# Fourier mixing from sums and differences of the sequence's halves: even and odd frequencies apart, each from half as many tokens

## The chip, the cores and the metric

The kernel runs on one core of a Trainium2 chip, all in f32. The metric is the device time of one execution in microseconds. The program computes several transformer blocks in a row on a sequence of 512 latent and 256 context tokens; the change concerns one short stage of the first block.

## The reference, cut to what matters

```python
FOURIER_WIDTH = 512; FOURIER_GROUPS = 4; FOURIER_GROUP_DIM = 128

def fourier_mix(u):                      # u: the first 512 columns of h @ w_in
    B_, L, _ = u.shape
    ug = u.reshape(B_, L, FOURIER_GROUPS, FOURIER_GROUP_DIM).astype(jnp.float32)
    f = jnp.fft.fft2(ug, axes=(1, 3), norm='ortho').real
    return f.reshape(B_, L, FOURIER_WIDTH).astype(u.dtype)
```

It is called once for the latent tokens (L = 512) and once for the context tokens (L = 256). The real part of the two-dimensional transform is cos(tokens) times cos(channels) minus sin(tokens) times sin(channels), which the kernel makes with matrix multiplications against tables.

## The kernel before

Activations lie transposed: channels on the 128 partitions, tokens along the free axis, 512 latent and behind them 256 context tokens, T = 768 together. The kernel is a row of stages. Each has one program for each engine and ends with a barrier of all engines.

`even_in` projects the normed input (25 jobs in `EV_JOBS`, in an order written out by hand). A job of the kinds z, q, k, v, u, r is one output tile of 128 channels: 8 matmuls of 512 and 8 of 256 columns (L1336, L1337) into one of three pairs of PSUM banks, and one ScalarE copy of 768 elements into SBUF (L1377). Jobs of the kind vt turn a value tile around (L1326), and VectorE copies them out (L1419); jobs g make the gates, on which VectorE has a chain of running sums behind the last one (L1394 to L1402, L1496). Job j waits only until the result of job j − 3 has been copied out. The four u tiles are the input of the Fourier mixing. The SP queue loads the projection's weights into three slots at the head of the region W, and behind the last of them the tables of the Fourier stage (L1302), over the same slots.

`fourier` works on four groups of 128 channels. `channels(g)` multiplies each of the 6 token tiles of a group with the 128-point table (L1450: 6 matmuls of 256 columns, cos and sin side by side). ScalarE copies the result into `G` (L1482), one of two buffers. `tokens(g)` sums over the token tiles with the tables of the sequence (L1460, L1461 for the latent, L1463, L1464 for the context tokens) into banks 6 and 7, and VectorE copies those into `A` (L1489). The order on TensorE is

```python
channels(0); channels(1)
for g in range(4):
    tokens(g)
    if g + 2 < 4:
        channels(g + 2)
```

`tokens(g)` waits for ScalarE's copy of its own group and for VectorE's copy of group g − 1, because there is one pair of result banks. `gla_scan` follows.

Of the kernel before, what the change touches and what calls it, by code (L numbers as in the profile page):

```python
# [19 lines left out]
MUL, ADD, SUB = ALU.mult, ALU.add, ALU.subtract  # L20

P = 128
D = 1024
KD = D // P
LAT, CTX = 512, 256
T = LAT + CTX
# [921 lines left out]
def pair_banks(ps, b, n):  # L948

    return ps[:, 2 * b:2 * b + 2, :].rearrange("p a c -> p (a c)")[:, 0:n]  # L950
# [281 lines left out]
EV_U = BIG  # L1232
# [21 lines left out]

def fourier_tables(m):
    at, W = m["at"], OFF["W"]
    return {"cos_lat": at(W, 4, LAT), "sin_lat": at(W + 4 * LAT, 4, LAT), "cos_ctx": at(W + 8 * LAT, 2, CTX),
            "sin_ctx": at(W + 8 * LAT + 2 * CTX, 2, CTX)}


def even_in(nc, m, io, feed, norm, early, mods):
# [4 lines left out]
    st, s = stage(nc, "evi", Norm.SEMS + "wg mm act ab gm ex ln ls cu mid ep en vt vtc own g gp" + mods.SEMS, {**feed.sems})  # L1266
    ps, at, cols = m["ps"], m["at"], m["cols"]
    wg = at(EV_WG, 2, 256)
    z, q, k, v = at(EV_Z, T), at(EV_Q, 2, T), at(EV_K, 2, T), at(EV_V, 4, T)
# [3 lines left out]
    released, tiles = {}, {}  # L1273
# [9 lines left out]
    def chunks(n):  # L1283
        return cum[:, n, :].rearrange("p (a c) -> p a c", c=RW_C)

    with st, nc.Block() as block:
        @block.sync
        def _(sp):
            sp.dma_start(wg[0:16, :, :], io["w_gla_gate"].rearrange("d r n -> r d n")).then_inc(s["wg"], 16)
            mods.begin(sp, s)  # L1290
            feed.rest(m, sp, s["mm"], lambda w: mods.between(sp, s, 0, w))
            sp.dma_start(at(GL_DFT, 2 * P), io["dft128"]).then_inc(early["dft"], 16)
            for name, dst in fourier_tables(m).items():
                n = dst.shape[1] * dst.shape[2]
                lo = {"cos_lat": 0, "sin_lat": 4 * LAT, "cos_ctx": 8 * LAT, "sin_ctx": 8 * LAT + 2 * CTX}[name]
                if lo < feed.slots * KD * P:
                    sp.wait_ge(s["mm"], feed.last_over(lo, lo + n))
                if lo + n > feed.slots * KD * P:
                    sp.wait_ge(s["mdm"], mods.N)
                if lo + n > EV_WG - OFF["W"]:  # L1300
                    sp.wait_ge(s["gp"], 4)
                sp.dma_start(dst, io[name].rearrange("(k p) n -> p k n", p=P)).then_inc(early["tab"], 16)  # L1302
# [82 lines left out]
        @block.vector  # L1385
        def _(dve):
            norm.dve(dve, s)
            own = Count(dve, s["own"])

            def centre(n):  # L1390
                last = RW_C - 1 if n < 2 else 0
                dve.wait_ge(s["cu"], n + 1)
                x = chunks(n)
                own.link(dve.tensor_scalar(ref[:, n, :], x[:, :, RW_C // 2], 1.0, None, MUL))  # L1394
                own.link(dve.tensor_tensor(fall[:, n, :], x[:, :, last], ref[:, n, :], SUB))
                dve.tensor_tensor(x, x, ref[:, n, :].rearrange("p (a c) -> p a c", c=1).to_broadcast([P, RW_NC, RW_C]), SUB
                                  ).then_inc(s["mid"], 1)

            def sums():
                for n in range(4):  # L1400
                    dve.wait_ge(s["ln"], n + 1)
                    dve.tensor_tensor(q_hat[:, n, :], q_hat[:, n, :], cum[:, n, :], SUB).then_inc(s["ls"], 1)  # L1402
                    dve.wait_ge(s["ls"], n + 1)
                    running_sum(dve, m["rst64"], q_hat[:, n, :], cum[:, n, :], n // 2).then_inc(s["cu"], 1)
                    if n:
                        centre(n - 1)
                centre(3)

            for j, (kind, i) in enumerate(EV_JOBS):
                x = pair_banks(ps, j % 3, T)  # L1410
                if kind == "g":
                    dve.wait_ge(s["ab"], i + 1)
                    dve.tensor_scalar(q_hat[:, i, :], x, bias(i), 0.0, ADD, ALU.min).then_inc(s["gm"], 1)
                    if i == 3:
                        dve.wait_ge(s["gm"], 4)
                        sums()
                if kind == "vt":
                    dve.wait_ge(s["vt"], i + 1)
                    dve.tensor_copy(vt[:, i, :, :].rearrange("p a c -> p (a c)"), x).then_inc(s["vtc"], 1)  # L1419
            mods.add(dve, s, 0)  # L1420
            e = RW_NC - 1
            own.done(dve.tensor_tensor(step[:, 0:2, 0:e], fall[:, 0:2, 0:e], ref[:, 0:2, 1:e + 1], ADD))
            own.done(dve.tensor_tensor(step[:, 0:2, e:e + 1], fall[:, 0:2, e:e + 1], ref[:, 0:2, 0:1], ADD))
            own.done(dve.tensor_tensor(step[:, 2:4, 1:e + 1], fall[:, 2:4, 1:e + 1], ref[:, 2:4, 0:e], ADD))
            own.link(dve.memset(step[:, 2:4, 0:1], 0.0))
            dve.memset(m["misc"][:, 31:32], 0.0).then_inc(s["g"], 1)
            for n in range(4):
                dve.wait_ge(s["ep"], n + 1)
                dve.scalar_tensor_tensor(q_hat[:, n, :], q[:, n % 2, :], 64.0 ** -0.5, q_hat[:, n, :], MUL, MUL)
                dve.wait_ge(s["en"], n + 1)  # L1430
                dve.tensor_tensor(cum[:, n, :], k[:, n % 2, :], cum[:, n, :], MUL)
            mods.add(dve, s, 1)


def fourier(nc, m, early):

    st, s = stage(nc, "fft", "g gc o oc", early)
    at, ps, A = m["at"], m["ps"], m["A"]
    ev = at(EV_U, 4, T)
    t = fourier_tables(m)  # L1440
    f = at(GL_DFT, 2 * P)
    G = at(EV_G, 2, TT, 2 * P)
    with st, nc.Block() as block:
        @block.tensor
        def _(pe):
            def channels(g):
                if g >= 2:
                    pe.wait_ge(s["gc"], g - 1)
                for t in range(TT):
                    mm = pe.matmul(ps[:, 3 * (g % 2) + t // 2, (t % 2) * 256:(t % 2) * 256 + 256], ev[:, g, t * P:(t + 1) * P], f,  # L1450
                                   start=True, stop=True)
                mm.then_inc(s["g"], 1)

            def tokens(g):
                x = G[:, g % 2, :, :]
                pe.wait_ge(s["gc"], g + 1)
                if g:
                    pe.wait_ge(s["oc"], g)
                for k in range(4):
                    pe.matmul(ps[:, 6, :], x[:, k, 0:P], t["cos_lat"][:, k, :], start=(k == 0), stop=False)  # L1460
                    pe.matmul(ps[:, 6, :], x[:, k, P:2 * P], t["sin_lat"][:, k, :], start=False, stop=(k == 3))  # L1461
                for k in range(2):
                    pe.matmul(ps[:, 7, 0:CTX], x[:, 4 + k, 0:P], t["cos_ctx"][:, k, :], start=(k == 0), stop=False)  # L1463
                    mm = pe.matmul(ps[:, 7, 0:CTX], x[:, 4 + k, P:2 * P], t["sin_ctx"][:, k, :], start=False, stop=(k == 1))  # L1464
                mm.then_inc(s["o"], 1)

            pe.wait_ge(s["dft"], 16)
            channels(0)
            channels(1)
            pe.wait_ge(s["tab"], 4 * 16)  # L1470
# [5 lines that stand above are left out]
        @block.scalar  # L1476
        def _(act):
            for g in range(4):
                act.wait_ge(s["g"], g + 1)
                if g >= 2:  # L1480
                    act.wait_ge(s["o"], g - 1)
                act.activation(G[:, g % 2, :, :].rearrange("p t c -> p (t c)"),  # L1482
                               ps[:, 3 * (g % 2):3 * (g % 2) + 3, :].rearrange("p a c -> p (a c)"), ACT.Copy).then_inc(s["gc"], 1)

        @block.vector
        def _(dve):
            for g in range(4):
                dve.wait_ge(s["o"], g + 1)
                dve.tensor_copy(A[:, g, :], pair_banks(ps, 3, T)).then_inc(s["oc"], 1)  # L1489


def running_sum(dve, reset, src, dst, backward):
# [2272 lines left out]
def shape_constants():  # L3765

    import numpy as np
    i = np.arange(P)
# [7 lines left out]
    g = np.arange(NE)  # L3776
# [7 lines left out]
    a = 2 * np.pi * np.outer(np.arange(P), np.arange(P)) / P  # L3784
    f["dft128"] = np.concatenate([np.cos(a), np.sin(a)], axis=1)
    for name, length in (("lat", LAT), ("ctx", CTX)):
        a = 2 * np.pi * (np.outer(np.arange(length), np.arange(length)) % length) / length
        f["cos_" + name] = np.cos(a) / np.sqrt(length * P)
        f["sin_" + name] = -np.sin(a) / np.sqrt(length * P)
    tok = np.arange(LAT)  # L3790
# [5 lines left out]
    i, j = i[:, None] % 64, np.arange(64)[None, :]  # L3796
# [82 lines left out]
```

## Time and profile before

| | |
|---|---|
| median of 3 runs | 3609.66 us (3606.34 to 3609.83) |
| span of the profiled execution | 3608.5 us |
| TensorE busy | 3331.8 us, 92% |
| VectorE busy | 1472.6 us, 41% |
| ScalarE busy | 920.5 us, 26% |
| GpSimd busy | 776.5 us, 22% |
| mean granted TensorE clock | 0.965 |
| projection and tables (`even_in`), about | until 261 us |
| Fourier stage | 262.1 to 311.2 us |

The profiled execution is given by its span, from its first to its last instruction; it has no other time of its own in the profile. In the profile PE is a TensorE matmul, PEld its weight load, DVE is VectorE, ACT ScalarE, SP the queue that issues loads. An f32 matmul of the code is two records, each with its own weight load. "PEclk" is the clock that TensorE was granted, as a part of full speed. Matmul records overlap by their drain: the pace is read from start to start.

### The profile page before, as it was taken

The page shows a single profiled execution, that of the slowest core. Times are in us where ns is not written, and L with a number is a line of the kernel's source. Part 1 is how long each engine was busy: PE and PEld are TensorE (multiplying, and loading weights), DVE is VectorE, ACT ScalarE, POOL GpSimd, SP SyncE. Part 2 cuts the span into 40 slices and gives each one's busy share as a digit, 9 for nine tenths or more (in the row PEclk, how much of TensorE's full clock was granted, in tenths as well). Part 3 has the DMA queues.
Part 4 walks back from the last instruction along what each step waited for, and adds up shares of the span by engine and source line. Part 5 has one row for each costly group of instructions (what it writes and reads, how often), then busy time and mean ns, then how long its engine had stood idle before and what let it go on. Part 6 is the DMA issues. An engine that isn't in the chain of part 4 may idle for free. (4 is left out here: it accounts for less than half of the span.)

```text
span 3608.5 us, 67939 instructions
## 1 busy us (share of the span) xinstructions
PE 3331.8 (92%) x27542; PEld 2255.2 (62%) x27542; DVE 1472.6 (41%) x3002; ACT 920.5 (26%) x1782; POOL 776.5 (22%) x727
## 2 busy tenths in 40 slices
PE   7999999999999999999999599989988899999984
PEld 3557555555555687787865289965775466655543
DVE  1213443345322454445266834434455233333324
ACT  2122232222002343222121433234322122222211
POOL 0000332223510024335410000003311233333320
PEclk9999999999999999999999599989999999999996
DMA  5330133312111003532211000001102799999996
GB/s 225 123 112 25 48 124 155 148 51 83 56 39 65 30 13 140 226 136 103 84 59 36 0 4 4 4 17 53 65 26 81 284 357 357 358 360 349 359 386 233
DMA packets 97639, 485.23 MB, mean 134 GB/s; under 512 B 16915, under 2 KB 21043, under 8 KB 53249
## 3 DMA queue, kind: packets, MB, share of 16 engines
q1 hardware_dynamic: 80880, 443.66, 33.4%
q0 software_dynamic: 16528, 38.25, 3.2%
q8 instruction: 176, 2.88, 0.3%
q14 instruction: 55, 0.44, 0.0%
HBM read 466.90 MB, written 31.46 MB: 138 GB/s over the span
## 5 line engine op out<-in xcount | busy, mean ns | idle before, releaser
L1011 PE MATMUL psum<-arena 128*128 128x384 f32 (+1 forms) x2464 | 674.4, 434 | 6.3 <-ACT arena L600 5.3
L1011 PEld LDWEIGHTS psum<-arena 128*128 128x128 f32 x2464 | 463.7, 189 | 221.3 <-issue 23.8
L842 PE MATMUL psum<-arena 128*128 128x256 f32 (+1 forms) x1904 | 511.6, 431 | 23.3 <-PEq L3092 10.0
L842 PEld LDWEIGHTS psum<-arena 128*128 128x128 f32 x1904 | 363.6, 191 | 171.8 <-issue 27.3
L3623 PE MATMUL psum<-arena 128*64 128x256 f32 x3072 | 352.6, 378 | 15.8 <-DMA arena<-exp_w_in 13.2
L3623 PEld LDWEIGHTS psum<-arena 128*64 128x64 f32 x3072 | 231.8, 134 | 161.4 <-issue 54.1
L453 POOL TENSOR_TENSOR arena<-arena 128x512 f32<-128x512 f32 x66 | 88.0, 1334 | 1054.9 <-POOLq L1671 365.7
L1139 DVE SCALAR_TENSOR_TENSOR arena<-arena 128x511 f32<-128x511 f32 (+1 forms) x264 | 177.0, 713 | 138.1 <-ACT arena L1117 135.0
L1089 ACT ACTIVATE arena<-psum 128x384 f32<-128x384 f32 (+1 forms) x176 | 76.3, 435 | 510.5 <-PE psum L1011 510.1
L462 POOL TENSOR_TENSOR arena<-arena 128x512 f32<-128x512 f32 (+1 forms) x74 | 114.6, 1549 | 395.6 <-PE psum L1011 245.6
L3637 PE MATMUL psum<-arena 128*64 128x512 f32 x768 | 185.3, 601 | 0.6 <-DMA arena<-exp_w_in 0.6
L1133 DVE TENSOR_TENSOR arena<-psum,arena 128x384 f32<-128x384 f32 (+1 forms) x132 | 64.6, 490 | 283.3 <-PE psum L1011 283.3
L2478 ACT ACTIVATE arena<-psum 128x256 f32<-128x256 f32 (+1 forms) x264 | 104.0, 422 | 240.2 <-PE psum L2327 62.1
L2796 PE MATMUL psum<-arena 128*128 128x384 f32 (+1 forms) x560 | 161.3, 449 | 4.1 <-ACT arena L600 4.0
L3717 DVE SCALAR_TENSOR_TENSOR arena<-arena,psum 128x128 f32<-128x128 f32 (+1 forms) x97 | 33.8, 349 | 281.0 <-ACT arena L3674 281.0
L563 POOL TENSOR_TENSOR arena<-arena 128x1536 f32<-128x1536 f32 (+1 forms) x3 | 11.3, 3766 | 636.3 <-ACT arena L600 636.3
L2796 PEld LDWEIGHTS psum<-arena 128*128 128x128 f32 x560 | 106.6, 191 | 59.5 <-ACT arena L600 7.9
L1336 PE MATMUL psum<-arena 128*128 128x512 f32 x272 | 140.7, 598 | 1.1 <-ACT arena L600 1.1
L3545 POOL TENSOR_TENSOR arena<-arena 128x1 f32<-128x1 f32 x195 | 39.8, 204 | 394.0 <-DVE arena L3712 379.4
L2039 PE MATMUL psum<-arena 128*128 128x512 f32 x240 | 116.6, 592 | 0.8 <-ACT arena L600 0.8
L2527 DVE TENSOR_TENSOR arena<-psum,arena 128x256 f32<-128x256 f32 x128 | 53.6, 424 | 130.7 <-PE psum L2459 39.5
L3562 POOL DMA_INDIRECT yrows<-arena x96 | 98.5, 1026 | 37.3 <-issue 37.3
(516 smaller groups left out, 5199.3 us busy)
## 6 DMA issues: line engine op xcount, KB each, us to landing
arena<-exp_w_in SPq DMA_DIRECT2D x207, 1024.0 KB
arena<-w_mod_r_in SPq DMA_DIRECT2D x72, 1024.0 KB, 7.0
arena<-w_ffn_up_in SPq DMA_DIRECT2D x44, 1024.0 KB, 4.8
arena<-w_ffn_down_in SPq DMA_DIRECT2D x32, 704.0 KB, 4.2
arena<-yrows SPq DMA_DIRECT2D x8, 2048.0 KB, 16.5
arena<-w_hgrn_in SPq DMA_DIRECT2D x10, 1024.0 KB
arena<-w_even_in_in SPq DMA_DIRECT2D x17, 512.0 KB, 3.6
arena<-w_in_in SPq DMA_DIRECT2D x15, 512.0 KB, 3.6
```

Source lines behind the costliest of these rows:

```text
L453: pool.tensor_tensor(s1, a21, a22, ADD).then_inc(s["ws"], 1)
L462: pool.tensor_tensor(a12, a12, self.piece(m, p, 5), SUB).then_inc(s["ws"], 1)
L842: mm = pe.matmul(pair_bank(ps, q, x, h), lhsT[:, k, :], rhs[:, k, :], start=(k == 0 and x in (1, 2, 7)), stop=(k == KH - 1), skip_group_ch ...
L1011: return pe.matmul(pair_bank(ps, q, x, h), feed.weights(m, q, x)[:, k, :], b.moving(x)[:, k, :], start=(k == 0 and x in (1, 2, 7)), stop=( ...
L1139: last = dve.scalar_tensor_tensor(y, x[:, lo + a:hi + e], column(q, v, tap), y, MUL, ADD)
L1336: pe.matmul(ps[:, 2 * b, :], lhsT, m["A"][:, x, 0:LAT], start=(x == 0), stop=(x == KD - 1))
L2039: mm = pe.matmul(ps[:, 2 * b, :], lhsT, m["A"][:, k, 0:LAT], start=(k == 0), stop=(k == KD - 1))
L2478: return act.activation(dst, src, ACT.Copy)
L2796: mm = pe.matmul(pair_bank(ps, i, x, h), lhsT[:, k, :], rhs[:, k, :], start=(k == 0 and x in (1, 2, 7)), stop=(k == 3), skip_group_check=x ...
L3562: pool.indirect_dma_start(io["yrows"], bass.IndirectOffsetOnAxis(ap=ids[:, u:u + 1].bitcast(U32), axis=0), y[u], None, bounds_check=LAT * ...
L3623: mm = pe.matmul(ps[64 * c:64 * c + 64, 0, 0:256], xt[u][:, k, :], wgu[w][:, k, :, c * P:(c + 1) * P], start=(k == 0), stop=(k == KD - 1))
L3637: mm = pe.matmul(ps[64 * c:64 * c + 64, 4, :], hT[:, j * 64:(j + 1) * 64], wdn[w][:, j, c * 512:(c + 1) * 512], start=(j == 0), stop=(j == 1))
```

## The change

The sequence's halves are combined before the transform. For even frequencies the kernel of the transform has the same value at tokens n and n + L/2, for odd ones the opposite value; so the even frequencies are a transform of the sum of the two halves, and the odd ones of their difference, each over L/2 tokens.

Behind the projection of each u tile VectorE writes the difference of the halves over the second half and then 2 x first half − difference, which is the sum, over the first half, for the latent and for the context tokens. The tables keep half of the rows, and their columns are sorted, the even frequencies first. `channels` is as it was: the transform over channels works on sums and differences alike. `tokens` makes the even frequencies from the tiles of sums and the odd ones from the tiles of differences. The copy out becomes two instructions, one for the latent and one for the context tokens, which write with a step of two elements and so put even and odd frequencies back in their order.

```diff
 def fourier_tables(m):
     at, W = m["at"], OFF["W"]
-    return {"cos_lat": at(W, 4, LAT), "sin_lat": at(W + 4 * LAT, 4, LAT), "cos_ctx": at(W + 8 * LAT, 2, CTX),
-            "sin_ctx": at(W + 8 * LAT + 2 * CTX, 2, CTX)}
+    return {"cos_lat": at(W, 2, LAT), "sin_lat": at(W + 2 * LAT, 2, LAT), "cos_ctx": at(W + 4 * LAT, 1, CTX),
+            "sin_ctx": at(W + 4 * LAT + CTX, 1, CTX)}
...
-                lo = {"cos_lat": 0, "sin_lat": 4 * LAT, "cos_ctx": 8 * LAT, "sin_ctx": 8 * LAT + 2 * CTX}[name]
+                lo = {"cos_lat": 0, "sin_lat": 2 * LAT, "cos_ctx": 4 * LAT, "sin_ctx": 4 * LAT + CTX}[name]
                 if lo < feed.slots * KD * P:
                     sp.wait_ge(s["mm"], feed.last_over(lo, lo + n))
                 if lo + n > feed.slots * KD * P:
...
                         sums()
+                if kind == "u":
+                    u = at(EV_U + i * T, T)
+                    dve.wait_ge(s["act"], tiles["u", i] + 1)
+                    for lo, mid, hi in ((0, LAT // 2, LAT), (LAT, LAT + CTX // 2, T)):
+                        own.link(dve.tensor_tensor(u[:, mid:hi], u[:, lo:mid], u[:, mid:hi], SUB))
+                        dve.scalar_tensor_tensor(u[:, lo:mid], u[:, lo:mid], 2.0, u[:, mid:hi], MUL, SUB)
                 if kind == "vt":
...
-                for k in range(4):
-                    pe.matmul(ps[:, 6, :], x[:, k, 0:P], t["cos_lat"][:, k, :], start=(k == 0), stop=False)
-                    pe.matmul(ps[:, 6, :], x[:, k, P:2 * P], t["sin_lat"][:, k, :], start=False, stop=(k == 3))
-                for k in range(2):
-                    pe.matmul(ps[:, 7, 0:CTX], x[:, 4 + k, 0:P], t["cos_ctx"][:, k, :], start=(k == 0), stop=False)
-                    mm = pe.matmul(ps[:, 7, 0:CTX], x[:, 4 + k, P:2 * P], t["sin_ctx"][:, k, :], start=False, stop=(k == 1))
+                for name, bank, first, tiles, half in (("lat", 6, 0, 2, LAT // 2), ("ctx", 7, 4, 1, CTX // 2)):
+                    for odd in range(2):
+                        part = slice(odd * half, (odd + 1) * half)
+                        for k in range(tiles):
+                            for j, table in enumerate(("cos_", "sin_")):
+                                mm = pe.matmul(ps[:, bank, part], x[:, first + odd * tiles + k, j * P:(j + 1) * P],
+                                               t[table + name][:, k, part], start=(k == 0 and j == 0),
+                                               stop=(k == tiles - 1 and j == 1))
                 mm.then_inc(s["o"], 1)
...
                 dve.wait_ge(s["o"], g + 1)
-                dve.tensor_copy(A[:, g, :], pair_banks(ps, 3, T)).then_inc(s["oc"], 1)
+                for bank, lo, hi in ((6, 0, LAT), (7, LAT, T)):
+                    o = dve.tensor_copy(A[:, g, lo:hi].rearrange("p (j a) -> p a j", a=2),
+                                        ps[:, bank, 0:hi - lo].rearrange("p (a j) -> p a j", a=2))
+                o.then_inc(s["oc"], 1)
...
     for name, length in (("lat", LAT), ("ctx", CTX)):
-        a = 2 * np.pi * (np.outer(np.arange(length), np.arange(length)) % length) / length
+        order = np.concatenate([np.arange(0, length, 2), np.arange(1, length, 2)])
+        a = 2 * np.pi * (np.outer(np.arange(length // 2), order) % length) / length
```

`own.link` sends an instruction and makes VectorE wait until it has finished.

## Rows read from the trace of the kernel before

**Rows 1.** The page, busy time and share of each engine:

```profile
PE 3331.8 (92%) x27542; PEld 2255.2 (62%) x27542; DVE 1472.6 (41%) x3002; ACT 920.5 (26%) x1782; POOL 776.5 (22%) x727
```

**Rows 2.** Timeline of TensorE in the Fourier stage: start, length, line, form, records:

```profile
262.15 7.00 PE L1450 MATMUL psum<-arena 128*128 128x256 f32 x24 [1.64 <-PEq L1286]
268.99 1.02 PE L1460 MATMUL psum<-arena 128*128 128x512 f32 x2
...
277.59 2.75 PE L1450 MATMUL psum<-arena 128*128 128x256 f32 x12
280.19 1.02 PE L1460 MATMUL psum<-arena 128*128 128x512 f32 x2
...
299.55 0.59 PE L1464 MATMUL psum<-arena 128*128 128x256 f32 x2
301.29 1.10 PE L1460 MATMUL psum<-arena 128*128 128x512 f32 x2 [1.14 <-DVE arena L1489]
...
312.55 0.45 PE L1571 MATMUL psum<-arena 64*64 64x64 f32 x8 [2.43 <-DVE arena L1649]
```

**Rows 3.** Timeline of ScalarE and VectorE in the Fourier stage:

```profile
269.19 1.45 ACT L1482 ACTIVATE arena<-psum 128x1536 f32<-128x1536 f32 x1 [1.14 <-PE psum L1450]
...
300.18 0.96 DVE L1489 COPY arena<-psum 128x768 f32<-128x768 f32 x1 [10.24 <-PE psum L1464]
```

**Rows 4.** Stretches of time: length, each engine's busy time, granted clock, DMA share, GB/s:

```profile
262.00:264.00 2.00, 1.85 (x5) 1.52 (x6) 0.00 (x0) 0.00 (x0) 0.00 (x0) 0.50 1.01 369
264.00:266.00 2.00, 2.00 (x8) 1.65 (x7) 0.00 (x0) 0.00 (x0) 0.00 (x0) 0.66 1.01 365
266.00:268.00 2.00, 2.00 (x11) 1.75 (x10) 0.00 (x0) 1.41 (x1) 0.00 (x0) 1.00 0.59 195
300.00:302.00 2.00, 0.86 (x3) 0.49 (x3) 0.96 (x1) 0.00 (x0) 0.00 (x0) 1.00 0.00 0
312.00:314.00 2.00, 1.45 (x34) 1.45 (x36) 0.79 (x3) 0.55 (x2) 0.00 (x0) 0.79 0.52 111
1225.00:1325.00 100.00, 99.98 (x678) 82.63 (x677) 55.05 (x122) 58.45 (x99) 0.00 (x0) 1.00 0.00 1
```

**Rows 5.** Timeline of TensorE in the attention stage:

```profile
1230.85 1.50 PE L1901 MATMUL psum<-arena 128*128 128x128 f32 x12
1232.19 1.02 PE L1892 MATMUL psum<-arena 128*128 128x512 f32 x2
```

**Rows 6.** Groups of VectorE instructions by line and form: busy us, mean ns:

```profile
L1646 DVE TENSOR_TENSOR arena<-arena 128x256 f32<-128x256 f32 x24 | 10.1, 421 | 6.2 <-PE psum L1593 6.2
L1633 DVE TENSOR_TENSOR arena<-psum,arena 128x128 f32<-128x128 f32 x24 | 6.9, 289 | 1.8 <-PE psum L1574 1.3
L3359 DVE TENSOR_TENSOR arena<-arena 128x256 f32<-128x256 f32 x1 | 0.5, 507 | 0.0
L3345 DVE TENSOR_TENSOR arena<-arena 128x256 f32<-128x256 f32 x1 | 0.4, 427 | 0.0
L3365 DVE COPY arena<-psum 128x64 f32<-128x64 f32 x1 | 0.2, 226 | 2.3 <-PE psum L3234 2.3
L1489 DVE COPY arena<-psum 128x768 f32<-128x768 f32 x4 | 3.8, 958 | 46.2 <-PE psum L1464 46.2
```

**Rows 7.** Timeline of VectorE and ScalarE in the projection:

```profile
179.76 0.96 DVE L1396 TENSOR_TENSOR arena<-arena 128x768 f32<-128x768 f32 x1
182.99 0.81 ACT L1377 ACTIVATE arena<-psum 128x768 f32<-128x768 f32 x1 [11.62 <-PE psum L1337]
185.46 0.96 DVE L1419 COPY arena<-psum 128x768 f32<-128x768 f32 x1 [4.74 <-PE psum L1326]
...
198.47 0.96 DVE L1419 COPY arena<-psum 128x768 f32<-128x768 f32 x1 [12.05 <-PE psum L1326]
```

**Rows 8.** Timeline of the SP queue at the projection's end:

```profile
258.09 0.39 SPq L1302 DMA_DIRECT2D arena<-cos_lat_in  x1
...
259.63 0.66 SPq L1302 DMA_DIRECT2D arena<-sin_ctx_in  x1
```

## The prediction

> **What bounds the kernel now.** I began with the page's busy shares: TensorE is busy for 92% of the span [rows 1], so work taken off its queue shows in the end unless something else ends last in its stage. The stage to look at is the Fourier mixing, 262 to 311 us. Its TensorE timeline [rows 2] is a straight line of instructions: 24 channel passes, then four times the token sums (one group of them 268.99 to 277.59), with the channel passes of groups 2 and 3 between. Every f32 multiplication stands there as two passes, so "x2" is one matmul of the code. The reader is to see that a line starts as the one before it runs out: TensorE waits for nobody, except ahead of the last group, where it stands from the end of group 2 to 301.29 for the VectorE copy that empties the two result banks. The other two engines are short next to it: the ScalarE copy of a group is 1.45 us, the VectorE copy 0.96 us [rows 3]. The granted clock is 0.50 when the stage begins, 1.00 from 266 us on, and stays 1.00 through the gap at 300 to 302 [rows 4]. So the stage is bound by the columns that TensorE streams. Its stages are closed by barriers: what it ends earlier, all later stages begin earlier.
>
> **Token sums: fewer columns.** One group now streams 8 matmuls of 512 columns and 4 of 256, that is 16 passes of 512 and 8 of 256, in 277.59 − 268.99 = 8.60 us [rows 2]. After the change the number of matmuls is the same, 12, and each has half the columns: 16 passes of 256 and 8 of 128. Their prices stand in the trace with the same 128x128 weights. The 12 channel passes of 256 columns run from 277.59 to 280.19, 0.217 us each [rows 2]; 12 passes of 128 columns in the attention stage run from 1230.85 to 1232.19, 0.112 us each [rows 5]. A group is then 16 x 0.217 + 8 x 0.112 = 3.47 + 0.89 = 4.36 us, 4.24 us less, and four groups give 16.96 us. The question is whether the weight load, which does not shrink (24 loads of 128x128 a group, before and after), sets a floor. A row says where it lies: 0.112 us at 128 columns is more than half of 0.217, but by little, so at 256 columns the load is covered, and at 128 just about. If on the contrary it took a 256-column time for each 128-column pass, the 32 such passes would cost 32 x (0.217 − 0.112) = 3.4 us more; that is the upper bound of this term.
>
> TensorE: Matmul & The Clock Gate, in the Trainium skill, section Back-to-back issue gap, speaks against the halving: it gives sustained pairs of load and matmul at about 81 ns for 128 columns where the bare matmul would be 56, because the load has to be paid as well. Taken as a factor of 1.45 on the bare half of my 256-column pass (an estimate), a 128-column pass would be 0.157 us and the change 32 x 0.045 = 1.4 us dearer; the row with 0.112 us is this kernel's own and is what the sum uses.
>
> **The order around them.** I followed the new schedule from the rows. Token sums 0 begin at 268.99 as now and end at 273.35. Channel passes 2 take 2.60 us, to 275.95; the ScalarE copy of group 1 is over at 270.64 [rows 3], so token sums 1 start at once. The copy of group 2 waits for its channel passes (275.95) and for token sums 0, and is over by 277.6, long before token sums 2 at 282.9; that of group 3 begins at about 282.9 and ends at 284.5, ahead of token sums 3 at 287.2 and later. So no ScalarE copy comes onto the path. Each copy has less room than before, but the least of it is over 2.5 us.
>
> **The copies out.** One VectorE copy of 768 elements (958 ns [rows 6]) becomes two, of 512 and 256, which write every second element so that even and odd frequencies interleave. From 958 ns at 768 and 226 ns at 64 elements [rows 6] an element is 1.04 ns and the fixed part 0.16 us: the pair costs 0.69 + 0.43 = 1.12 us, 0.16 more. Behind groups 0 and 1 it lies beside 2.60 us of channel passes, so nothing is seen; without that cover it would be twice 1.1 us. Behind groups 2 and 3 it is on the path: 2 x 0.16 = 0.32 us. The trace has no copy with a step of two elements. Nearest is L3359, which writes every third element: 507 ns for 256 where its neighbour with contiguous writes has 427 [rows 6], 0.31 ns an element. By that the pair is 0.24 us dearer, 0.48 for the two on the path. A gain is excluded, a step cannot be faster than none. I take 0.1 a copy, the lower side, since two elements' step is closer to the contiguous row, and keep 0 and 0.48 for the range.
>
> The Trainium skill, SBUF — State Buffer, section Door 1: The DMA port swizzle, says that lines are 16 bytes wide and that a stream runs at full rate while it hits a line at least twice. A step of two f32 hits twice, L3359's step of three does not always. By that the term is 0 here, against 0.48 by the row; the trace agrees as far as L3359 pays.
>
> **The new VectorE work in the projection.** For each of the four u tiles VectorE adds a difference and a sum over 256 elements, then the same over 128: 2 x 0.42 + 2 x 0.29 = 1.42 us [rows 6], with two short waits on itself about 1.5, so 6 us in all. I cost it at nothing. What hides it: VectorE's queue ends its running sums at about 180.7, u0 is long there, and the next thing behind it is the vt copy at 185.46, before which VectorE stands idle for 4.74 us. For u1 the ScalarE copy ends at 183.8, so VectorE is free again at about 185.3, just before that vt copy [rows 7]. The later u tiles repeat this every 13.0 us (185.46 to 198.47 [rows 7]). If it ran late by a few tenths, the vt copy would free a bank that TensorE wants only three projection tiles on, over 10 us later. And the stage's end is set by the last projection tile, done by 258.09 [rows 8]. Without that cover the cost would be those 6 us.
>
> **The tables.** The four loads were 2.5 MB, issued from 258.09 when the last projection tile is done [rows 8], and were still moving after 266 (DMA share 0.59 in 266 to 268 [rows 4]); the token sums want them at 268.99. They become 1.25 MB. The first now overwrites only the first weight slot and may go one tile earlier; the other three wait as before. All land sooner. Nothing was waiting for them, so the gain is 0; no queue has anything moved in front of it. Two of the waits that SP had there fall away, and SP has ended before the barrier either way.
>
> **The sum.** 16.96 − 0.32 − 0.2 = 16.4 us. The profiled span of 3608.5 becomes 3592.1. The median of the runs, 3609.66, stands 1.2 above that span; the same difference on it gives 3593.2 us.
>
> **Rivals.** First, the narrow passes do not run at 0.112 us between weight loads of alternating tables: for it speaks that nothing in this stage streams 128 columns yet and that each pass meets a load as long as itself; against it, that the 12 of [rows 5] load new weights each pass too. Up to 3.4 us back: 3596.6. The rule of the Trainium skill quoted above, the same page and section, is a milder case of this rival.
>
> Second, the clock drops in the gap ahead of the last group. That gap is 1.3 us now and would be about 1.6; the clock held at 1.00 through it [rows 4], but after the gap of 2.43 us at the stage's end [rows 2] it is 0.79 in 312 to 314. Token sums 3 at half clock cost 4.36 us more: 3597.6. Against it stands also the attention stage, which with its 128-column passes has 1.00 for 100 us [rows 4].
>
> Third, on the other side: the clock does not rise at all in this stage and stays at its 1.2 GHz level, after shorter stretches of streaming than now. Then the token sums are 4 x 8.72 = 34.9 us against 34.4 now, channel passes 2 and 3 are 2.6 us dearer each, and the first 24 go from 6.84 to 24 x 0.433 = 10.4: 0.5 + 5.2 + 3.6 + 0.5 for the copies = 9.8 us slower, 3619.5. It decides from the point at which some 16.4 us of full-speed work runs at half. Against it stands that the clock rises at 264 to 266 during the channel passes, which the change does not touch [rows 4].
>
> **How the numbers follow.** The forecast has 0.80, the first rival 0.06, the second 0.09, the third 0.02, and 0.03 lies with what I do not see. The predicted time is the forecast's. Its own range: the three runs spread over 3606.3 to 3609.8, so 3606.3 less 17 gives 3589.3, and 3609.8 less 15.9 (stepped writes at the full 0.48, no other loss) 3593.9. For such differences between runs I allow a little more: 3588 below. Above it reaches over both smaller rivals, 3596.6 and 3597.6, to 3599. A measurement of this kernel tells about 0.2%, 7.2 us, from no change; the forecast and the first two rivals are beyond that (3602.4), the third rival is slower.
>
> **What would show it.** The token lines should show 16 passes at 0.21 to 0.22 and 8 near 0.11 a group, some 4.4 us from the first to the next channel line; the two copies about 1.1 to 1.3 us together; the scan's first matmul near 296 instead of 312.55; the projection's TensorE line unchanged until 258; and the DMA quiet by 262 or so. The prediction is wrong if TensorE shows waits for VectorE inside the projection, if the granted clock after 270 is under 1.00, or if the copies run beyond 2 us.

## The result, and the profile after

| | before | after |
|---|---|---|
| median | 3608.0 us (3604.58 to 3609.83, 4 runs) | 3587.97 us (3585.96 to 3589.61, 4 runs) |
| ratio | | 0.9946, 95% interval 0.9934 to 0.9958 |
| span of the profiled execution | 3608.5 us | 3587.7 us |
| first channel pass to first matmul of the scan | 312.55 − 262.15 = 50.40 us | 295.75 − 262.11 = 33.64 us |

The four runs of the kernel before are the three that the forecast started from and one more. The change makes the kernel faster by about 0.5%. The forecast was 3593.2 us, a gain of 16.4 us. The Fourier stage itself gave 16.76 us; the spans of the two profiles differ by 20.8. So there are two questions: whether the stage went as forecast step by step, and where the other 4 us are from.

TensorE's timeline in the changed kernel, to be read beside [rows 2] (L1456 is the channel transform, L1470 the token sums, L1582 the scan's first line):

```profile
262.11 7.11 PE L1456 MATMUL psum<-arena 128*128 128x256 f32 x24 [1.64 <-PEq L1286]
269.06 4.51 PE L1470 MATMUL psum<-arena 128*128 128x256 f32 x24
273.41 2.76 PE L1456 MATMUL psum<-arena 128*128 128x256 f32 x12
276.00 4.51 PE L1470 MATMUL psum<-arena 128*128 128x256 f32 x24
280.35 2.76 PE L1456 MATMUL psum<-arena 128*128 128x256 f32 x12
282.95 4.51 PE L1470 MATMUL psum<-arena 128*128 128x256 f32 x24
288.67 4.59 PE L1470 MATMUL psum<-arena 128*128 128x256 f32 x24 [1.21 <-DVE arena L1498]
295.75 0.45 PE L1582 MATMUL psum<-arena 64*64 64x64 f32 x8 [2.49 <-DVE arena L1660]
```

The order is the same and no new wait has come. A group of token sums takes 273.41 − 269.06 = 4.35 us where it took 8.60. The only wait for VectorE is still that ahead of the last group.

A line names only one form of its group: 16 of the 24 passes have 256 columns, 8 have 128. The timeline cut late in group 0 shows the last seven of the 128-column passes by themselves:

```profile
272.63 0.94 PE L1470 MATMUL psum<-arena 128*128 128x128 f32 x7
273.41 0.38 PE L1456 MATMUL psum<-arena 128*128 128x256 f32 x1
```

That is 273.41 − 272.63 = 0.78 us for seven, 0.111 each.

VectorE's groups in the stage, by line and form (busy us, mean ns), and its timeline at one u tile of the projection, to be read beside [rows 6] and [rows 7]:

```profile
L1498 DVE COPY arena<-psum 128x512 f32<-128x512 f32 x4 | 2.8, 692 | 29.2 <-PE psum L1470 29.2
L1498 DVE COPY arena<-psum 128x256 f32<-128x256 f32 x4 | 1.7, 415 | 0.0
```

```profile
183.79 0.43 DVE L1421 TENSOR_TENSOR arena<-arena 128x256 f32<-128x256 f32 x1 [1.79 <-ACT arena L1377]
184.25 0.43 DVE L1422 SCALAR_TENSOR_TENSOR arena<-arena 128x256 f32<-128x256 f32 x1
184.60 0.28 DVE L1421 TENSOR_TENSOR arena<-arena 128x128 f32<-128x128 f32 x1
184.91 0.29 DVE L1422 SCALAR_TENSOR_TENSOR arena<-arena 128x128 f32<-128x128 f32 x1
185.42 0.96 DVE L1425 COPY arena<-psum 128x768 f32<-128x768 f32 x1 [0.21 <-PE psum L1326]
```

The four new instructions fill the 1.4 us between the end of ScalarE's copy and the vt copy, with 0.21 us of idle time left: the vt copy starts at 185.42 where it started at 185.46.

The SP queue (beside [rows 8]) and stretches of time (beside [rows 4]: length, busy time of PE, PEld, DVE, ACT, POOL, then the granted clock, DMA share, GB/s):

```profile
246.89 0.43 SPq L1302 DMA_DIRECT2D arena<-cos_lat_in  x1
258.06 0.37 SPq L1302 DMA_DIRECT2D arena<-sin_lat_in  x1
```

```profile
262.00:264.00 2.00, 1.89 (x7) 1.64 (x8) 0.00 (x0) 0.00 (x0) 0.00 (x0) 0.79 0.01 3
264.00:266.00 2.00, 2.00 (x7) 1.55 (x6) 0.00 (x0) 0.00 (x0) 0.00 (x0) 0.50 0.00 0
...
288.00:290.00 2.00, 1.33 (x6) 1.22 (x7) 0.53 (x2) 0.00 (x0) 0.00 (x0) 1.00 0.00 0
...
296.00:298.00 2.00, 2.00 (x56) 2.00 (x53) 1.01 (x3) 0.56 (x2) 0.00 (x0) 1.00 0.96 283
```

The DMA is quiet from 262 us on; in [rows 4] it was still at work after 266. The clock holds through the gap at 288 as it did before. The scan runs at full clock from its start, which it did not before: behind the row of 312 to 314 in [rows 4], the profile of the kernel before has

```profile
314.00:316.00 2.00, 2.00 (x23) 2.00 (x21) 0.72 (x2) 0.00 (x0) 0.00 (x0) 0.50 0.98 401
```

From the scan's first matmul to the first one of the stage behind it (L1677 before, L1688 after) it is 361.64 − 312.55 = 49.08 us before and 343.20 − 295.75 = 47.45 after, with the same instructions: 1.63 us. The remaining 2.3 us lie in the rest of the kernel, 3246.8 us before and 3244.5 after, which the change does not touch.

### The profile page after: what moved, and what is told of

Its sections match the earlier page's. It is cut to its first block and busy times, and to the rows that moved or that the text cites. A ratio compares the mean times of both kernels' runs of the same rounds, so it can differ in the third digit from the quotient of the medians.

```text
span 3587.7 us, 67958 instructions
## 1 busy us (share of the span) xinstructions
PE 3314.3 (92%) x27542; PEld 2250.5 (63%) x27542; DVE 1477.9 (41%) x3022; ACT 921.7 (26%) x1782; POOL 778.1 (22%) x727
```

## The experiments

Two theories on the part beyond 16.8 us, by the TensorE clock that was granted; a low stretch is one in which it was 0.50. **Theory A:** TensorE's low-clock stretches fall elsewhere in each execution, and the two profiles happened to differ. **Theory B:** the low stretch behind the Fourier stage belongs to the long stage, and the short one is rid of it for good. Beside them: is VectorE's new work really free, does the stepped write cost anything, and what is left in the stage.

**e1: the kernel before, profiled again.** No edit.

> The kernel before, unchanged, profiled a second time. Theory A (the part of the gain beyond the Fourier stage is the position of the granted clock's low stretches, different in each execution): the stages up to the Fourier stage's end agree with the first profile within 0.3 us except where a low stretch lies elsewhere, the low stretch at the start of the scan (313.1 to 316.6 in the first profile) may be there or not, and the span lies anywhere in 3604 to 3611. Theory B (the low stretch behind the Fourier stage belongs to the long stage of before): it is there again, at the same place within 1 us, and the scan stage is again about 44.4 us.

Measured: 3606.4 us over 10 runs beside 3606.23 over 21 (ratio 1.0, 0.9991 to 1.0009). Stage (first channel pass to the scan) 50.39, scan 49.08, as in the first profile, rest 3244.7. Theory B forecast this, and theory A allowed it. It also shows that the median of the kernel before over 21 runs is 3606.23: the median of the three runs that the forecast started from lay 3.4 us above that. (The expectations count the stages between other bounds: the 47.2 and 45.6 us of the scan there stand beside 49.08 and 47.45 here, and 50.0 and 33.3 us of the Fourier stage beside 50.40 and 33.64. The 44.4 us in the expectation of e1 fits neither count.)

**e2: the changed kernel, profiled again and timed five times.** No edit.

> The changed kernel, unchanged, profiled a second time and timed in five rounds. Both theories: the Fourier stage ends 16.8 us earlier than before (first matmul of the scan at 295.8 within 0.3 us, apart from clock). Theory A: the low stretches lie elsewhere than in the first profile of it, one may fall on the scan's start (then 297 to 301 runs at half clock and the scan stage is 1.6 us longer); the ratio over five rounds is about 1 - 16.8/3608 = 0.9953, a gain of 15 to 20 us. Theory B: the scan starts at full clock again and the ratio is about 0.9948 (18.5 us or more).

Measured: 3588.78 us (3587.78 to 3590.74) beside 3606.23, ratio 0.9953 (0.9939 to 0.9966), a gain of 17.4 us. The first 24 channel passes took longer here, at half clock until 268 us, so that the stage took 297.20 − 262.30 = 34.90 us; the scan 47.45. The ratio is the one that theory A gave, but its interval holds the 0.9948 of theory B too, so it decides nothing.

**e3: VectorE's new work alone**, in the kernel before:

```diff
+                if kind == "u":
+                    u, w = at(EV_U + i * T, T), at(EV_G, T)
+                    dve.wait_ge(s["act"], tiles["u", i] + 1)
+                    for lo, mid, hi in ((0, LAT // 2, LAT), (LAT, LAT + CTX // 2, T)):
+                        own.link(dve.tensor_tensor(w[:, mid:hi], u[:, lo:mid], u[:, mid:hi], SUB))
+                        own.link(dve.scalar_tensor_tensor(w[:, lo:mid], u[:, lo:mid], 2.0, w[:, mid:hi], MUL, SUB))
```

> The kernel before with nothing of the change but VectorE's sums and differences behind each u tile, written to a place that no one reads. Theory (hidden work): 0 us, the projection's TensorE timeline ends at 258.0 as before, ratio 0.9995 to 1.0005. Rival (it delays the copies of the turned value tiles and TensorE with them): up to 6 us later, ratio 1.0015.

Measured: 3606.49 us over 10 runs, ratio 1.0002 (0.9993 to 1.0011). The first channel pass stands at 262.11 (262.15 before), and TensorE has no wait from 170 to 258 us, as before. The work is hidden. And a surprise: this kernel has the long Fourier stage (51.69 us, a longer low stretch at its start), but its scan started at full clock and took 47.45 us:

```profile
313.80 0.45 PE L1577 MATMUL psum<-arena 64*64 64x64 f32 x8 [2.43 <-DVE arena L1655]
...
314.79 0.61 PE L1588 MATMUL psum<-arena 64*64 64x128 f32 x8
```

The same form took 1.07 us at half clock in e1:

```profile
312.38 0.45 PE L1571 MATMUL psum<-arena 64*64 64x64 f32 x8 [2.42 <-DVE arena L1649]
...
313.68 1.07 PE L1582 MATMUL psum<-arena 64*64 64x128 f32 x8
```

That is against theory B.

**e4: copies out without the step**, in the changed kernel; the frequencies are left unsorted.

```diff
-                    o = dve.tensor_copy(A[:, g, lo:hi].rearrange("p (j a) -> p a j", a=2),
-                                        ps[:, bank, 0:hi - lo].rearrange("p (a j) -> p a j", a=2))
+                    o = dve.tensor_copy(A[:, g, lo:hi], ps[:, bank, 0:hi - lo])
```

> The changed kernel with its two copies out written contiguously: the even and odd frequencies are left unsorted. If the step of two elements costs as the step of three does in L3359 (0.31 ns an element), the pair falls from 1.02 to about 0.78 us and the scan starts 0.5 us earlier; if it costs nothing, the pair stays at 1.02 us and the scan's first matmul at 295.75.

Measured in the timeline of VectorE:

```profile
281.04 1.02 DVE L1498 COPY arena<-psum 128x512 f32<-128x512 f32 x2 [5.93 <-PE psum L1470]
```

1.02 us as with the step, and the stage took 296.23 − 262.59 = 33.64 us, as in the changed kernel. The step of two elements costs nothing here. The total, of a single run, 3625.19 us, is not that of this work: behind the scan it has 35 us more and 69053 instructions instead of 67958, presumably because what the experts' loops have to do depends on what was computed. It was not followed further.

**e5: the last group's sums in banks of their own**, in the changed kernel:

```diff
-                if g:
+                if 0 < g < 3:
                     pe.wait_ge(s["oc"], g)
-                for name, bank, first, tiles, half in (("lat", 6, 0, 2, LAT // 2), ("ctx", 7, 4, 1, CTX // 2)):
+                base = 6 if g < 3 else 0
+                for name, bank, first, tiles, half in (("lat", base, 0, 2, LAT // 2), ("ctx", base + 1, 4, 1, CTX // 2)):
...
-                for bank, lo, hi in ((6, 0, LAT), (7, LAT, T)):
+                for bank, lo, hi in ((6 if g < 3 else 0, 0, LAT), (7 if g < 3 else 1, LAT, T)):
```

> The changed kernel with the last group's token sums in banks 0 and 1, which the channel transform has left by then, so that they don't wait for VectorE's copy of group 2. If the 1.21 us of idle TensorE time ahead of the last group is that wait and nothing else: it goes, the last group's first pass starts 4.35 us after that of group 2, and the Fourier stage takes 33.3 - 1.3 = 32.0 us. Rival (something else, such as the ScalarE copy of group 3, ends right behind it): less than 0.5 us.

Measured:

```profile
283.05 8.87 PE L1471 MATMUL psum<-arena 128*128 128x256 f32 x48
294.41 0.45 PE L1583 MATMUL psum<-arena 64*64 64x64 f32 x8 [2.49 <-DVE arena L1661]
```

The last two groups are one line of 48 passes. The stage took 294.41 − 262.21 = 32.20 us, 1.44 less than 33.64. The wait was VectorE's copy and nothing ended right behind it.

**e6: e5, and the latent copy made while TensorE sums the context tokens:**

```diff
+                    if name == "lat":
+                        mm.then_inc(s["ol"], 1)
...
-                dve.wait_ge(s["o"], g + 1)
                 for bank, lo, hi in ((6 if g < 3 else 0, 0, LAT), (7 if g < 3 else 1, LAT, T)):
+                    dve.wait_ge(s["o" if lo else "ol"], g + 1)
```

> As the kernel before this one, and VectorE copies the latent part of each group as soon as the latent sums are done, while TensorE makes the context sums (0.9 us). At the stage's end only the context copy (0.43 us) is left of the pair's 1.02: the Fourier stage takes 32.0 - 0.6 = 31.4 us, 1.9 us less than in the changed kernel. In the total that is 0.05%, less than five rounds can tell: ratio to the kernel before 0.9948 with theory A and the changed kernel's 0.9953.

Measured:

```profile
284.03 8.87 PE L1471 MATMUL psum<-arena 128*128 128x256 f32 x48
294.80 0.45 PE L1585 MATMUL psum<-arena 64*64 64x64 f32 x8 [1.90 <-DVE arena L1663]
```

From the first pass of group 2 to the scan it is 10.77 us, in e5 11.36 and in the changed kernel 295.75 − 282.95 = 12.80: 2.03 us less than in the changed kernel, of which 0.59 are the early copy. The total does not show it: 3590.29 us (3588.53 to 3592.36, 5 runs) beside 3606.98, ratio 0.9954 (0.9940 to 0.9968), where the changed kernel had 0.9953. The profiled execution had the longer low stretch at the stage's start and 3246.4 us behind the scan. So e6 is better in its stage and not shown to be better in time.

**e7: VectorE's work three times**, twice into a place that no one reads, in the changed kernel:

```diff
+                    w = at(EV_G, T)
+                    for _ in range(2):
+                        for lo, mid, hi in ((0, LAT // 2, LAT), (LAT, LAT + CTX // 2, T)):
+                            own.link(dve.tensor_tensor(w[:, mid:hi], u[:, lo:mid], u[:, mid:hi], SUB))
+                            own.link(dve.scalar_tensor_tensor(w[:, lo:mid], u[:, lo:mid], 2.0, w[:, mid:hi], MUL, SUB))
```

> The changed kernel with VectorE's sums and differences made three times for each u tile, twice into a place that no one reads: 4.6 us instead of 1.4 between the end of a u tile and the vt copy behind it in VectorE's queue. The vt copies start 3 us later (188.4, 201.4 and 214.4 instead of 185.42, 198.43 and 211.44). Theory (over 10 us of cover): TensorE's timeline in the projection does not change, the last projection tile is done at 258.0, and the stage takes 219.0 us as before. Rival (TensorE needs the vt copy's bank or its data at once): up to 9 us more.

Measured:

```profile
189.50 0.95 DVE L1430 COPY arena<-psum 128x768 f32<-128x768 f32 x1
...
201.24 0.95 DVE L1430 COPY arena<-psum 128x768 f32<-128x768 f32 x1
```

The vt copies start 4.1 and 2.8 us later than in the changed kernel (the expectation had 3; the first is later because u0's work runs into u1's). TensorE still has no wait from 170 to 258 us, the first channel pass stands at 262.06, and the stage takes 33.64 us. The cover holds three times the work.

**e8: the kernel before, a third profile.** No edit.

> The kernel before once more, for a third profile of it. Theory A (position of the low stretches): the scan stage takes 47.2 us if a stretch at half clock falls on its start, as in two profiles of this kernel so far, or 45.6 if none does, as in the profile of the kernel with VectorE's work alone; the Fourier stage takes 50.0 us if the clock comes up once at about 265.4, and about 51.3 if it comes up at 268. Theory B (the low stretch behind the Fourier stage belongs to the kernel before): 47.2 us again.

Measured: the scan took 47.45 us, the stage 314.14 − 262.57 = 51.57, with the clock at half until 268:

```profile
266.00:268.00 2.00, 2.00 (x6) 1.55 (x6) 0.00 (x0) 0.00 (x0) 0.00 (x0) 0.50 0.85 289
```

```profile
314.14 0.45 PE L1571 MATMUL psum<-arena 64*64 64x64 f32 x8 [2.43 <-DVE arena L1649]
...
315.12 0.61 PE L1582 MATMUL psum<-arena 64*64 64x128 f32 x8
```

The kernel before, without any edit, has a scan at full clock in one execution and not in two others, after the same gap of 2.43 us. So the low stretch doesn't belong to the long stage as such, and theory B as stated has fallen. Whether the long stage makes it likelier is another question, taken up below the table.

**e9: the kernel before, with TensorE busy in the gap ahead of the scan:** two multiplications of 512 columns behind the last token sums, into a bank that no one reads.

```diff
                 if g + 2 < 4:
                     channels(g + 2)
+            busy(pe, m, 4, 2)
```

> The kernel before with two multiplications of 512 columns (1.7 us) behind the last token sums, into a bank that no one reads, so that TensorE streams while VectorE makes the last copy and the gap ahead of the scan falls from 2.4 to about 0.8 us. If the low stretch at the scan's start comes from that gap: it is gone, the scan stage takes 45.6 us instead of 47.2, and the Fourier stage grows by 0.5 to 0.8 us, since TensorE comes to the barrier later than VectorE's copy. Rival (the low stretch has to do with what ran before the gap): 47.2 us still.

Measured: scan 47.45 us, stage 314.35 − 262.19 = 52.16, with the longer low stretch at the stage's start. The gap ahead of the scan fell to 1.41 us, not to the 0.8 expected. The scan is as expected, but e8 has the same without the added work. The run therefore tells nothing on the cause; only its cost stands, 0.6 us in the stage against e8 and 0.7 behind the first 24 channel passes.

**e10: the changed kernel, a third profile.** No edit.

> The changed kernel once more, for a third profile of it. Both theories: Fourier stage 33.3 us with one short low stretch at its start, 34.5 with a longer one. Theory A: the scan stage takes 45.6 us, or 47.2 if a low stretch falls on its start, which none of six profiles with the short stage has shown. Theory B: 45.6 us.

Measured: stage 296.86 − 262.25 = 34.61 us, with the longer low stretch at its start, scan 47.44.

All profiles together, in us. The second column is the first without its first 24 channel passes, on which the low stretch at the stage's start falls; "behind" is all behind the scan:

| | stage | of it behind the first 24 passes | scan | behind |
|---|---|---|---|---|
| before | 50.40 | 43.56 | 49.08 | 3246.8 |
| e1, before again | 50.39 | 43.55 | 49.08 | 3244.7 |
| e8, before again | 51.57 | 43.56 | 47.45 | 3243.9 |
| e3, VectorE's work alone | 51.69 | 43.55 | 47.45 | 3240.5 |
| e9, before, busy at the end | 52.16 | 44.26 | 47.45 | 3245.7 |
| after | 33.64 | 26.69 | 47.45 | 3244.5 |
| e2, after again | 34.90 | 26.70 | 47.45 | 3241.4 |
| e10, after again | 34.61 | 26.70 | 47.44 | 3244.6 |
| e7, work thrice | 33.64 | 26.70 | 47.45 | 3244.7 |
| e4, plain copies | 33.64 | 26.69 | 47.45 | 3279.6, other work |
| e5, own banks | 32.20 | 25.25 | 47.45 | 3244.4 |
| e6, own banks, early copy | 32.52 | 24.67 | 47.45 | 3246.4 |

Stages whose low stretch at the start is short differ by 50.40 − 33.64 = 16.76 us, and those with the longer one by about 16.9 (means 51.63 and 34.76). Behind the first 24 passes nothing of this is left: 43.56 − 26.70 = 16.86 us, within 0.01 us in every profile of either kernel. That is what the change gives at full clock.

In no profile with the short stage, seven with e4, e5 and e6, did a low stretch fall on the scan's start; it did in two of five with the long one. Those two are the ones in which the low stretch at the stage's start was short, and the three others had the longer one. So with the long stage the two low stretches went together in these five profiles, while the short stage had a scan at full clock after either. Whether the change therefore saves some of the 1.6 us on average, or this is chance, is open.

What lies behind the scan varies by 6.3 us with the same instructions, more than the 2.3 us that the first two profiles differ by. Much of it goes with the granted clock. Read in stretches of 10 us, the time behind the scan in which the clock was missing (length times what it lacks of 1.00) is 111.3 us in the shortest execution (e3) and 123.3 and 126.1 in the two longest (before, e6). Over the eleven profiles with the same work the correlation of the two is 0.82; e8, with 111.6 and 3243.9, shows that it isn't everything. That supports theory A for the total; it does not say what moves the stretches.

## Why the prediction was right, step by step

**Token sums.** Right. 4.35 us a group against the 4.36 forecast; four groups gave 4 x (8.60 − 4.35) = 17.0 us. The passes of 128 columns run at 0.111 us, as in the attention stage [rows 5]; the first rival, up to 3.4 us back, did not come. Nor did its milder form at 0.157 us, which the prediction drew from the Trainium skill (TensorE: Matmul & The Clock Gate, section Back-to-back issue gap).

The prediction asked where the weight load sets a floor, and took 0.112 us as the sign that it is just covered. The kernel before has narrower f32 passes with 128x128 weights that settle it, both at a granted clock of 1.00:

```profile
1124.31 1.39 PE L1765 MATMUL psum<-arena 128*128 128x1 f32 x12
1125.56 1.11 PE L1795 MATMUL psum<-arena 128*128 128x512 f32 x2
...
2759.94 1.00 PE L3257 MATMUL psum<-arena 128*128 128x64 f32 x8
2760.78 1.08 PE L3264 MATMUL psum<-arena 128*128 128x512 f32 x2
```

A pass of one column takes (1125.56 − 1124.31) / 12 = 0.104 us and one of 64 columns (2760.78 − 2759.94) / 8 = 0.105 us. The floor lies there, and the 128-column passes stand almost on it. This halving was paid in full; halving the context passes once more would give almost nothing. Whether the floor is the weight load or another fixed cost of a pass isn't separated by any run.

**The schedule.** Right: group 1 starts at 276.00 (forecast 275.95), channel passes 3 at 280.35, group 2 at 282.95 (282.9), and no copy by ScalarE is on the path: those of groups 2 and 3 end at 277.65 and 284.60, over 4 us ahead of the token sums that read them.

**The copies.** Right in place, too dear in size. The forecast had 1.12 us for the pair by adding both fixed parts, plus 0.1 for the step; measured are 1.02 and nothing for the step, as e4 shows. Each copy took what was forecast (692 and 415 ns), but the second begins before the first is through, so the pair is 0.09 us shorter than their sum. The copies on the path cost 2 x 0.06 = 0.12 us instead of 0.52. The row of L3359 [rows 6] is no measure for a step of two elements, and it also reads one operand in another form than its neighbour, so that its 80 ns aren't shown to be the step's. The Trainium skill's rule of 16-byte lines (SBUF — State Buffer, section Door 1: The DMA port swizzle) gave the right size here: 0 for a step of two, as in e4. No run tests it at a step of three.

**The sum for the stage.** 17.0 − 0.12 − 0.11 (the first 24 channel passes took 6.95 us instead of 6.84) = 16.8 us, measured 16.76, forecast 16.4. Without those first passes, whose time goes by the clock, it is 16.86.

**VectorE in the projection, and the tables.** Right, both cost nothing: e3 and e7 show it for the first, with cover for three times the work. For the tables there is only the trace: the first load is issued at 246.89, the DMA is quiet by 262, and TensorE had not waited for them before.

**The clock.** The second and third rival did not come: 1.00 through the gap at 288 and in every stretch of the stage from 268 on. What the prediction left out of its single number is that the low stretches elsewhere move from one execution to the next. The measured median lay 5.2 us under the forecast one. The kernel before had itself come down by 1.7 us against the number that the forecast started from, with the fourth run, and 0.4 are the stage. The remaining 3.1 I put down mostly to the small number of runs: with 21 runs before and five after (e2) the gain was 17.4 us, 1.0 above the forecast and 0.6 above the stage's 16.8, inside an interval of 12 to 22. That the runs differ by the low stretches fits the profiles, as above, but isn't shown run by run.

**The range.** The median stands 0.03 us below the lower end that the prediction gave (3587.97 against 3588), for these reasons and not for a step in the stage; that it came so close to the edge is the start value's doing. The forecast started from three runs whose median was 3.4 us above that of 21. The upper sum of the range has a slip: with stepped writes at 0.48 the gain is 16.96 − 0.32 − 0.48 = 16.2 us and not 15.9, which took the 0.2 off as well. It gives 3593.6 instead of 3593.9 and changes nothing, since the range reaches further for the rivals.

## What to carry to other kernels

Where a stage's TensorE timeline is one unbroken line, its time is columns: find the price of a pass of the new width elsewhere in the same trace, with the same weights' shape, and multiply. An algebraic halving pays in full down to the floor of a pass. Here that is 0.104 us even for one column, so 128 columns (0.111 us) are the last width that pays. Look for the narrowest passes in the trace before halving further. The sums that a halving needs can lie on an engine that is idle in the stage before; check what is queued behind them. For a change worth 0.5% compare the stage in the two traces, from its first to the next stage's first instruction, at equal clock; the total carries several us that move from one execution to the next, here largely with the granted clock.

## What the runs showed of the hardware

- The same instructions of the scan stage took 49.08 us or 47.45, and the Fourier stage 50.40 or 51.57, in executions of one unchanged kernel, by where the granted clock was 0.50. What lies behind the scan took from 3243.9 to 3246.8 us in the kernel before and from 3241.4 to 3244.6 in the changed one.
- VectorE's f32 copy out of PSUM costs the same with writes at a step of two elements as with contiguous ones: 1.02 us for the pair of 512 and 256 in both (e4). The one instruction with a step of three took 80 ns more for 256 elements than its neighbour [rows 6]; no run isolates the step there.
- Two such copies in a row take 0.09 us less than the sum of their times (692 + 415 ns against 1.02 us).
- A chain of f32 passes, each with its own load of 128x128 weights, takes at full clock 0.217 us a pass at 256 columns, 0.111 at 128, 0.105 at 64 and 0.104 at one column.
